# Where a decoder step places six of its gate and branch matmul pieces: between the paged attention groups, or behind the last of them

## The reference, cut to what matters

```python
h = rmsnorm(x) ; z = h @ w_in            # q, k, v of both branches, and the gates ga, gm
att = moba(qa, ka, va, cache_k, cache_v, page_table)   # sampled tokens: 8 batches x 16 pages of 128 rows
ml  = mlstm(qm, km, vm, ...)
u   = sigmoid(ga) * (att @ w_attn_br) + sigmoid(gm) * (ml @ w_mlstm_br)
x   = x + rmsnorm(u @ w_out)
y   = x + rmsnorm(square(relu(rmsnorm(x) @ w_up)) @ w_down)
```

## Time and profile before

| | |
|---|---|
| median of three runs | 1126.72 us |
| the profiled execution's own time | 1128.49 us |
| its span, from first to last instruction | 1126.9 us |
| TensorE busy over the span | 1073.0 us (95%) |
| VectorE, ScalarE, GpSimd busy | 50%, 40%, 11% |
| mean granted TensorE clock | 0.978 of full speed |
| middle of the decode (slots 8 to 31) | from 411.7 to 569.1 us |
| tail of the decode (slots 32 to 39) | from 569.1 to 608.4 us |

### The profile page before, as it was taken

How to read it: one execution, slowest core, us unless ns; L and a number is a source line. 1 busy time by engine, 2 the same in 40 slices (tenths; PEclk the granted TensorE clock), 3 DMA queues, 4 the chain that set the end, 5 groups by cost and what they waited for, 6 DMA issues and landing times.

```text
span 1126.9 us, 21173 instructions
## 1 busy us (share of the span) xinstructions
PE 1073.0 (95%) x7577; PEld 916.5 (81%) x7577; DVE 563.3 (50%) x1226; ACT 449.5 (40%) x1022; POOL 125.9 (11%) x226
## 2 busy tenths in 40 slices
PE   3999999999999999999999995999999999999997
PEld 2988877887877877777789884998899899889985
DVE  5253523644765665566555657244344334433456
ACT  5254213333555465555552355242233213322451
POOL 4002210221001023333330100000000000000000
PEclk7999989999999999999999997999999999999999
DMA  6342214325115889999964531222222222222222
GB/s 204 89 120 58 56 38 122 70 72 147 47 39 153 261 279 338 337 339 335 338 200 135 158 117 47 74 77 85 84 75 83 84 82 76 84 84 82 79 85 84
DMA packets 93704, 149.84 MB, mean 133 GB/s; under 512 B 9377, under 2 KB 39590, under 8 KB 93622
## 3 DMA queue, kind: packets, MB, share of 16 engines
q1 hardware_dynamic: 75040, 103.83, 30.0%
q0 software_dynamic: 11968, 39.85, 10.4%
q10 hardware_dynamic: 6614, 5.06, 1.6%
HBM read 141.62 MB, written 7.10 MB: 132 GB/s over the span
## 4 chain that ended last, share of the span: by engine, by line
PE 79%; DVE 8%; issue 4%; DMA 3%; ACT 3%; SPq 1%; ACTq 1%; POOLq 0%; POOL 0%; DVEq 0%
PE ps L460 27%; PE ps L485 19%; PE ps L853 7%; PE ps L1860 4%; PE ps L468 4%; PE ps L869 4%; PE ps L433 2%; DMA kring<-in_cache_k_dram 2%; PE ps L1901 2%; PE ps L1869 2%; DMA w<-in_w_in_dram 1%; PE ps L1017 1%; PE ps L1037 1%; PE ps L1885 1%; DVE xn L533 1%
## 5 line engine op out<-in xcount | busy, mean ns | idle before, releaser
L345 DVE TENSOR_TENSOR w<-w,w 128x512 fp32r<-128x512 f32 (+1 forms) x240 | 168.2, 707 | 317.5 <-ACT w L334 312.9
L334 ACT ACTIVATE w<-w 128x512 fp32r<-128x512 f32 (+1 forms) x240 | 145.3, 613 | 362.6 <-PE ps L468 185.1
L485 PE MATMUL ps<-h2T,w 128*128 128x288 f32 x1536 | 210.5, 298 | 4.4 <-DVE h2T L2257 2.1
L485 PEld LDWEIGHTS ps<-h2T,w 128*128 128x128 f32 x1536 | 207.8, 190 | 7.1 <-DVE wide L2466 2.4
L460 PE MATMUL ps<-w,hid 128*128 128x512 f32 x672 | 161.6, 389 | 0.0
L460 PE MATMUL ps<-w,hT 128*128 128x512 f32 x576 | 148.5, 408 | 1.0 <-ACT ri L774 1.0
L460 PEld LDWEIGHTS ps<-w,hid 128*128 128x128 f32 x672 | 125.9, 188 | 26.1
L460 PEld LDWEIGHTS ps<-w,hT 128*128 128x128 f32 x576 | 108.2, 194 | 26.6 <-issue 4.3
L853 PE MATMUL ps<-hT,w 128*128 128x288 f32 x768 | 126.8, 307 | 0.0
L853 PEld LDWEIGHTS ps<-hT,w 128*128 128x128 f32 x768 | 105.1, 188 | 12.3 <-issue 11.6
L1827 POOL DMA_DIRECT2D vring<-in_cache_v_dram x128 | 68.8, 538 | 170.9 <-issue 170.9
(11 more groups left out here) (349 smaller groups left out, 1281.2 us busy)
## 6 DMA issues: line engine op xcount, KB each, us to landing
kring<-in_cache_k_dram SPq DMA_DIRECT2D x128, 256.0 KB, 4.0
vring<-in_cache_v_dram POOLq DMA_DIRECT2D x128, 256.0 KB, 4.4
w<-in_w_in_dram SPq DMA_DIRECT2D x88, 256.0 KB, 2.9
w<-in_w_up_dram SPq DMA_DIRECT2D x64, 256.0 KB, 2.7
w<-in_w_down_dram SPq DMA_DIRECT2D x64, 256.0 KB, 2.6
w<-in_w_out_dram SPq DMA_DIRECT2D x16, 256.0 KB, 2.8
x<-in_x_prompt_dram SPq DMA_DIRECT2D x4, 512.0 KB, 7.4
out_dram<-sC ACTq DMA_DIRECT2D x1, 2048.0 KB
```

The source lines that it names most:

```text
L334: eng.activation(spread(w_hi, n, j, width), together(w32, n, j, width), ACT.Copy)\
L345: eng.tensor_tensor(spread(w_lo, n, j, width), together(w32, n, j, width), spread(w_hi, n, j, width).bitcast(F32), ALU.subtract).then_inc( ...
L485: mm = eng.matmul(ps[:, b, 0:HALFT], w[a][:, j, i * P:(i + 1) * P], right[c][:, k, h * HALFT:(h + 1) * HALFT], start=(k == 0 and (c, a) == ...
```

## The change

It alters the table of pieces only. Slots 8, 12, 16, 20, 24 and 28 get two pieces and not one. Slots 32 to 39 get 2, 1, 1, 2, 1, 1, 2, 0: one less in each of slots 32 to 37. The sum is the same, and so is the order of the pieces.

```diff
@@ def pieces_in(s):
         if s < VALS:
             return 2
         if s < ALL_GROUPS:
-            return 1
-        return (3, 2, 2, 3, 2, 2, 2, 0)[s - ALL_GROUPS]
+            return 2 if s % 4 == 0 else 1
+        return (2, 1, 1, 2, 1, 1, 2, 0)[s - ALL_GROUPS]
```

## The result

The changed kernel is slower. It took 1136.54 us in the median of seven runs (1132.87 to 1140.65) against 1127.39 us before; the ratio is 1.0073, with a 95% interval of 1.0045 to 1.0099. Three more series of runs of this kernel, of which the last two shared a chip, gave 1.0067 (1.0046 to 1.0088), 1.0073 (1.0046 to 1.0100) and 1.0059 (1.0035 to 1.0083). The forecast was +2.5 us with a range up to 1132.6 us. So the direction was right, the time lies outside the range, and the size was missed by a factor of three.

The account below looks back on a forecast made before the run. TensorE was taken to bound both middle and tail of the decode. The middle's +6.2 us less the tail's 3.7 gave +2.5 us on the median of 1126.72, so 1129.2 us, range 1125.2 to 1132.6 us.

Parts of the forecast that it names:

- what the tail gives: Slots 32 on: values 31 come 2.9 us earlier and 30 matmuls follow instead of 36, 0.8 us less; 3.7 us gained.
- the middle's price: Slots 8 to 31: six second pieces cost 9.5 us, 5.3 us of waits go, 2.0 us of stalls remain; +6.2 us.
- let the waits for keys go: Middle: TensorE's 1.9 us of waits for pages of keys were taken to vanish, pages having 1.59 us more to arrive.
- the bounds, 4.2 and 9.5: Middle: growth is 4.2 us if every wait goes and 9.5 us if none does.
- the loop of the values up to group 29: Tail: GpSimd fetches values only after the group two before is used; group 28 lands at 584.6, group 29 at 589.7.
- The forecast waits of 4, 1 to 2 and 2 us: Tail: TensorE should wait this long for values (`vring`) at groups 28, 29 and 31.
- The pause of GpSimd: Rival, chance 0.26: the 2.73 us pause in group 28's pages does not recur; tail gives 5.8 us, total 1127.1 us.
- group 31 starts to be fetched 2.42 us after values 29 begin: Tail: from there 3.72 us to its last page and 3.5 to land, so values 31 come at 599.3, 2.9 us earlier.
- It waits 4 us: Tail: TensorE, ready at about 580.5, waits for group 28's last page, landing at 584.6.
- The stalls that stay: Rival, chance 0.12: pages of keys keep the middle's 5.3 us of stalls; middle costs 9.5 us, total 1132.5 us.
- The rule that a piece would hide in the middle: Rival, chance 0.05: weight loads fill 74% of TensorE's middle, so extra matmuls hide; sum -3.7 us, 1123.0 us.
- the row: Profile row on how long a values page takes to land: 3.5 us median, 2.9 least; preferred to the skill's 2.6.

Follow-up runs that it names:

- again2: The changed kernel once more, unaltered, for a third profile and more times; median 1136.06 us.
- again: The changed kernel once more, unaltered; median 1136.23 us.
- again3: The changed kernel once more, unaltered, for a fourth profile and more times; median 1134.13 us.
- tail_alone: Against the kernel before: slots 8 to 31 keep one piece each, slots 32 to 39 get 2, 1, 1, 2, 1, 1, 8, 0; median 1141.14 us, ratio 1.0122.
- waits_filled: The changed kernel plus unread matmuls ahead of the products with values, 20, 6, 6 and 14 in slots 34 to 37; median 1133.78 us.
- The filled kernels: Two kernels: the changed kernel plus unread matmuls ahead of the products with values in slots 34 to 37, fewer or more; medians 1133.78 and 1136.26 us.
- the kernels with early values: SyncE loads values of groups 28 and 29 early: changed table 1128.64 us, extra pieces one slot later 1126.11, old table 1128.25, six tail pieces moved to slot 38 1135.42.

## Why the prediction was wrong

The forecast was 1129.2 us, and the 25 runs of the changed kernel average 1135.3. Of the 6.1 us between them, 1.9 are the base (1126.72, the median of three runs, where 74 runs average 1128.6), 0.5 the middle, 2.8 the tail, and 0.9 stay open. The term that failed is what the tail gives: 3.7 us in the sum, 0.9 by the profiles.

**Right in its sum, in part by luck: the middle's price.** The step said 9.5 - 5.3 + 2.0 = 6.2 us, and five profiles against seven say 6.7. TensorE's busy time rose by 163.86 - 154.52 = 9.3 us. ScalarE's stall in slot 13 fell to 0.34 where 0.39 was worked out, the tanh included. But the step let the waits for keys go, and on average they stayed at 2.8 us of 3.6; ScalarE's gave back more than was priced, 2.2 us and not 1.4, from a higher base. The two nearly cancel. What the step did not see is that its base was a lucky execution: against that one profile the growth is 8.2 us, and pages of keys vary by 4 us from one execution to the next. Against the mean of the old middles all seven lie within the bounds, 4.2 and 9.5; against the one profile again2's 170.1 lies 10.2 above.

**Right: the loop of the values up to group 29.** Values 28 began 15.37 us after slot 32, forecast 15.5; values 29 20.67, forecast 20.6. The forecast waits of 4, 1 to 2 and 2 us came as 3.34, 1.11 and 2.35. The pause of GpSimd came again, with 3.43 us in this profile and in those of again, again2, again3, tail_alone and waits_filled, so that rival falls.

**Wrong: "group 31 starts to be fetched 2.42 us after values 29 begin".** By then GpSimd was still issuing group 30, since it never gets ahead: its first page of group 31 left at 599.62, not at 596.48 + 2.42 = 598.9, and the last landed 3.9 us after it left, not 3.5. TensorE also waited 1.03 us for group 30, which the step had left out. Values 31 began 31.46 us after slot 32 and not 30.2. With the clock whole the tail gave 2.2 us (36.9 against a mean of 39.1 in the three profiles with the old tail) and not 3.7: 1.5 us of the miss.

**Wrong: a wait was priced at its own length.** The prediction read a full clock in the tail from the earlier trace rows, where TensorE is busy for 37.6 of 39.3 us, and kept it in a tail where it forecast some 8 us of waiting. "It waits 4 us" had no term behind it. The runs show one: behind the wait of 3.4 to 3.6 us the clock goes to half in three of four profiles of the changed kernel and the tail then takes up to 40.9 us; the four tails average 38.2, so the tail gave 0.9 us, and the clock has the other 1.3 us of the miss. The timed runs agree on the direction: their loss to the clock rose from 20.7 to 24.2 us (by 3.6 and 3.1 beside before in the same set), and the remainder by 3.1. These 3 us and more are the upper bound, of which the profiles turn under half into time. The filled kernels tie the falls to the idle time, and the kernels with early values tie the slowdown to the late values.

**The rivals.** The stalls that stay, 1132.5 us, ended nearest in time but not in kind: ScalarE's stall went, and keys were waited for somewhat less than before. The rule that a piece would hide in the middle, because loads of weights fill only three quarters of it, was refuted by the 9.3 us of busy time and the middle's 6.7. A landing took 3.3 us in the median of the changed tail (569 to 612 us), nearer to the row than to the estimate of 2.6 us from the figures of the Trainium skill ("DMA: Bandwidth & Descriptors", "Anatomy of one DMA — SWDGE (gpsimd) path").

**Open.** The middles and tails of the four profiles of the changed kernel sum to 5.8 us over before, the means of the timed runs differ by 6.7, the ratios say 6.7 to 8.2. The four profiled executions average 1134.2 us, 1.1 below the mean of the runs, which may be all of it; where the slow ones lose their clock was not seen. The share of the clock in the miss, 1.3 us, rests on four profiles. Why the clock falls in one execution and holds in the next was not found, nor why GpSimd pauses between the first two pages of group 28; of the latter only this is seen, that one packet of the instruction queue moved in the same microseconds in the profiles of before and after (none did in that of tail_alone).

## What to carry to other kernels

Before work is taken out of a stretch, ask what it was covering there: here the transfers behind it ran at the issuing engine's pace, with nothing in hand (TensorE already waited 0.30 us for group 29), and six pieces of filler were their cover. A new wait of TensorE of some microseconds (3.5 here) is not to be priced at its length alone; look whether the granted clock falls behind it, and in more than one profile; then read what this costs from the length of the stage, since time x (1 - clock) was over twice the real cost here. And take the base of a sum from several executions where a view shows waits for DMA engines that are busy all the time: one profile of the middle was 2.1 us below the mean of five.

## What was not expected of the hardware

- A fall of TensorE's clock can start from a single wait in the midst of busy stretches: 2.46, 3.40, 3.48 and 3.55 us of idle time were followed by 1.2 GHz, 3.34 us in another execution was not, nor 3.00 later in the tail of again. Matmuls behind it took 1.7 to 1.8 times as long.
- The same kernel, unaltered, spread over 10 us (1123.25 to 1133.09 in 34 runs), and its time went with its mean granted clock: 0.985 in the shortest, 0.976 in the longest.
- GpSimd's DMAs of 256 KB left 1.24 us apart at the least in the changed tail, about 5.0 us for a group of four; SyncE issued the same pages while GpSimd issued others, and with that alone the changed tail took 30.7 us in place of 36.8 and more.
